# Attention's fill steps of an even unit all stand between its first and its second group of turned rows

## The chip, the cores and the metric

The kernel runs on one core of one Trainium2 chip. The metric is the device time of one execution in microseconds; the median of three timed runs is given, and one further execution was profiled.

## The reference, cut to what matters

Two layers, each with four token mixers beside each other on a sequence of 1024 tokens and a model width of 1024. Mixer A is softmax attention in a band, mixer C softmax attention over selected keys (here: all keys up to the query's tile, with a bias that masks those not selected). Both have four heads of width 64:

```python
# A: each 64-token chunk sees its own and 8 previous chunks
s = einsum('bnqhd,bnkhd->bhnqk', qc, kb) * dh ** -0.5 + bias
o = einsum('bhnqk,bnkhd->bnqhd', softmax(s), vb)
# C: the 256 best keys of an indexer
s = einsum('bqhd,bqkhd->bhqk', qb, ksel) * dh ** -0.5
o = einsum('bhqk,bqkhd->bqhd', softmax(s), vsel)
# both are multiplied by silu(z), projected, gated with sigmoids and summed
y = sum(sigmoid(g_b) * (o_b @ w_branch[b])); x = x + y @ w_out
```

B and D are recurrences in chunked form. All input projections and the sixteen blocks of gate columns are one matrix product `h @ w_in`, and that is most of the work.

## The kernel before, in words

All five engines run one program each, with semaphores between them. The order within an engine is written out by hand, and the engines run through the mixers in the order C, D, B, A, twice (two layers).

**Fills.** The large product `h @ w_in` is not a stage of its own. It is cut into *steps*, and `pe_fill(pe, n)` puts the next n steps into TensorE's stream wherever the hand-written order asks for them. During both attentions a step is one fp32 matmul of 128x128 by 128x512, which the profile shows as two MATMUL records of line 474. Four steps make a *product*: it accumulates in one of the two PSUM banks G, and when its last step is done ScalarE takes it out (lines 528, 537, 541, 547), for some products followed by a tanh (line 559) and a store. Seven products of this kind (`PRODUCTS`, p = 0 to 6) make one block of 256 columns. The lists of fills are handed to ScalarE by number: `act_ready(key)` first takes out every product that had ended, in TensorE's program order, when the job `key` was issued, and only then waits for `key` itself. So the place of a fill in TensorE's order also sets its place in ScalarE's order.

**Attention.** A *unit* u is one tile of 128 queries and one head; there are 32 (tile u // 4, head u % 4). TensorE's loop (line 1039 and after) takes for an even u the scores of units u and u+1 together (line 1003), into two double banks S2. VectorE adds the bias and takes the maximum (line 1102), line 1107 negates it, ScalarE takes the exponential (line 1083) and marks `probs`. TensorE then transposes ("turns") the probabilities of unit u in groups of at most four 128x128 tiles (line 1014), and ScalarE copies each group from PSUM (line 1069); then the values product follows (line 1027). There is one bank T for all turned groups, so a group can only be written when ScalarE has copied the one before it. In iteration u the loop turns the rows of unit u-1. A unit has a second group (`rest`) when it spans more than four key tiles. In mixer C unit u spans u // 4 + 1 tiles, so tiles 4 to 7 have a second group of 1 to 4 tiles; in mixer A it spans at most 5, so tiles 4 to 7 have a second group of one tile. Each finished tile is scaled and turned again through T (`oT`, line 1062).

In both mixers, VectorE's work on unit u waits for the last turned group of unit u-2 (it writes into the same buffer).

ScalarE's loop (line 1064 and after), in iteration u: copy of the first group of unit u-1; exponential of unit u; copy of the second group of unit u-1.

```python
ATT_FILL = {"A": 2, "C": 1}
ODD_FILL = {"A": 0, "C": 1}
```

Of the kernel before, what the change touches and what calls it, by code (L numbers as in the profile page):

```python
# [38 lines left out]
SEMS = 150  # L39
SMALL = 473  # L40

ATT_FILL = {"A": 2, "C": 1}
ODD_FILL = {"A": 0, "C": 1}
IDX_FILL = 1
A_FILL = 54
# [127 lines left out]
def gated_merge_kernel(nc, x, w_in, w_branch, w_out, params, toep, consts, cos_sin, a_mask, final_g, out):  # L173
    ctx = ExitStack()
    with ctx:
# [18 lines left out]
        C = lambda name: con[:, CONST[name][0]:CONST[name][1]]  # L194
# [41 lines left out]
        def sg(name):  # L236

            if name not in named:
                named[name] = ctx.enter_context(nc.semaphore(name))
            return named[name]  # L240
# [13 lines left out]
        for l in range(DEPTH):  # L254
# [52 lines left out]
            def next_unit():  # L307

                if todo:
                    b, js = todo[0]  # L310
                    free = fill_after.get((b, js[0])) is None or fill_after[b, js[0]] in jobs.at
                    if free:
                        todo.pop(0)
                        add_projection(b, js)
                        return True
                if gates[0] < len(gate_order):
                    add_gate()
                    return True
                return False

            def unit_at(key):

                return unit_of["gate", key[1]] if key[0] == "gate" else unit_of.get(key[:2])
# [96 lines left out]
            def pe_fill(pe, n):  # L420

                for _ in range(n):
                    if fill_at[0] == len(fills) and not next_unit():
                        return
                    key, blk, c, p = fills[fill_at[0]]
                    if unit_at(key) is None:
                        pe_fill_direct(pe, key, blk, c, p)
                    else:
                        pe_fill_product(pe, unit_at(key), key, c, p)
# [6 lines left out]
            def pe_fill_direct(pe, key, blk, m, c):  # L436

                slot, kt = 2 + blk % 2, fill_at[1]
                if kt == 0:
                    jobs.open(pe, key, next_g())  # L440
                    pe.wait_ge(sg(f"fill_w_loaded{blk % 2}"), 16 * (blk // 2 + 1))
                ap = jobs.at[key][0].ap
                ins = pe.matmul(ap, lhsT=wr[:, slot, kt, P * m:P * m + P], rhs=hT[:, kt, 512 * c:512 * c + 512],
                                start=kt == 0, stop=kt == KT - 1)
                fill_at[1] = kt + 1
                if kt == KT - 1:
                    pe_fill_ended(ins, key)

            def pe_fill_product(pe, u, key, i, p):

                h_side, w_side, fresh = PRODUCTS[p]
                kt = fill_at[1]
                if kt == 0:
                    jobs.open(pe, key, next_g())
                    if p == 0 and not i:
                        k = units[u][1][0]
                        pe.wait_ge(sg(f"fill_w_loaded{k % 2}"), 16 * (k // 2 + 1))
                    if p == 2 and u == 0:
                        pe.wait_ge(sg("h_sums"), 3)
                    if p == 3 and u == 0:  # L460
                        pe.wait_ge(sg("h_sums"), 5)
                    if w_side == "t2" and i == 0 and is_rows(u):
                        pe.wait_ge(sg("w_half_sums"), 2 * rows_units(u) + 2)
                    elif w_side in FIRST_T and not i:
                        pe.wait_ge(sg("w_sums"), 4 * u + FIRST_T[w_side])
                if is_rows(u) and w_side == "t2" and i == 0 and kt == half_k // 2:
                    pe.wait_ge(sg("w_sums"), 4 * u + 2)
                ap = jobs.at[key][0].ap
                if is_rows(u):
                    for kt in (kt, kt + 1):  # L470
                        ins = pe.matmul(ap[:, 0:NCB], lhsT=left(h_side, kt)[:, P * i:P * i + P], rhs=right(u, w_side)[:, kt, :],  # L471
                                        start=fresh and kt == 0, stop=kt == half_k - 1, skip_group_check=True)
                else:
                    ins = pe.matmul(ap, lhsT=right(u, w_side)[:, kt, :], rhs=left(h_side, kt), start=fresh and kt == 0,  # L474
                                    stop=kt == half_k - 1, skip_group_check=True)
                fill_at[1] = kt + 1
                if kt == half_k - 1:
                    pe_fill_ended(ins, key)
# [489 lines left out]
            def attention(b, q, k, v, z, first_tile, bias, at_s, at_pt, v_unit=None, each_unit=None, act_unit=None, masked=False):  # L968
# [7 lines left out]
                def span(u):  # L976
                    i, h = units[u]
                    k0 = first_tile(i)
                    return i, h, k0, i + 1 - k0
# [4 lines left out]
                def groups(nb):  # L984
                    return [(g, min(4, nb - g)) for g in range(0, nb, 4)]
# [10 lines left out]
                def scores(pe, u):  # L996

                    i, h, k0, nb = span(u)
                    aps = [jobs.open(pe, ("S", b, u + e), S2[e]) for e in range(2)]
                    for c in range(0, P * nb, 512):  # L1000
                        w = min(512, P * nb - c)
                        for e in range(2):
                            ins = pe.matmul(aps[e][:, c:c + w], lhsT=head(q, h + e, P * i, P * i + P),  # L1003
                                            rhs=head(k, h + e, P * k0 + c, P * k0 + c + w), start=True, stop=True)
                            if c + w == P * nb:
                                jobs.filled(ins, ("S", b, u + e))

                def turn(pe, u, group):

                    g, n = group  # L1010
                    key = ("PT", b, u, g)
                    ap = jobs.open(pe, key, T)
                    for j in range(n):
                        ins = pe.transpose(ap[:, P * j:P * j + P], rows[u % 2][:, P * (g + j):P * (g + j) + P], ident)  # L1014
                    jobs.filled(ins, key)
# [21 lines left out]
                def pe(pe):  # L1037
                    for u in range(len(units) + 2):
                        if u < len(units) and u % 2 == 0:
                            scores(pe, u)  # L1040
                        if 1 <= u <= len(units):
                            pe.wait_ge(sg("probs_" + b), u)
                            turn(pe, u - 1, groups(span(u - 1)[3])[0])
                        rest = groups(span(u - 1)[3])[1:] if 1 <= u <= len(units) else []
                        if u % 2 == 0:
                            pe_fill(pe, ATT_FILL[b])
                        elif not rest:
                            pe_fill(pe, ODD_FILL[b])
                        if u >= 3 and u % 2 == 1:
                            values(pe, u - 3)  # L1050
                        for group in rest:
                            turn(pe, u - 1, group)
                        if u % 2 == 0:
                            pe_fill(pe, ATT_FILL[b])
                        if u >= 5 and u % 4 == 1:
                            pe_fill(pe, 1)
                            i = u // 4 - 1
                            key = ("oT", b, i)
                            ap = jobs.open(pe, key, T)
                            pe.wait_ge(sg("z_scaled_" + b), i + 1)  # L1060
                            for m in range(2):
                                ins = pe.transpose(ap[:, P * m:P * m + P], z[:, i, P * m:P * m + P], ident)
                            jobs.filled(ins, key)
# [1270 lines left out]
```

## Time and profile before

| | us |
|---|---|
| median of 3 runs (2878.49 to 2882.49) | 2880.6 |
| the profiled execution | 2881.09 |
| its span in the trace | 2879.3 |
| TensorE busy in the span | 2790.9 (97%) |
| VectorE, ScalarE, GpSimd busy | 1584.4, 967.6, 819.7 |

The span runs from the first to the last recorded instruction; 1.8 us of the profiled time lie around it. "Busy" of TensorE contains modelled ends, so that a row's duration overlaps the start of the next row; the distance between two starts is what an instruction costs on TensorE. The attention of mixer C lies at about 350 to 458 us in layer 0 and 1785 to 1893 us in layer 1, that of mixer A at about 1059 to 1176 and 2492 to 2607 us.

### The profile page before, as it was taken

To read this page: it belongs to the slowest core of one execution; us is meant where nothing else is said; L and a number is where in the kernel's file an instruction comes from. 1 tells how busy PE (TensorE), PEld (TensorE's weight loads), DVE (VectorE), ACT (ScalarE), POOL (GpSimd) and SP (SyncE) were. 2 spreads that over 40 slices of the span, in tenths; PEclk is the share of its full clock that TensorE was granted. 3 is DMA by queue.
4 is the path that set the end of the run, shared out by engine and by line. 5 is a ranking of instruction groups with operands and counts; after the bars stand their busy time and mean duration, and the time that the engine had idled before them with its cause. 6 is when DMAs were issued, how large, how long until landed. Compare 5 with 4: busy or idle time off the path is not lost. (4 is left out here: it accounts for less than half of the span.)

```text
span 2879.3 us, 45819 instructions
## 1 busy us (share of the span) xinstructions
PE 2790.9 (97%) x18640; PEld 1493.9 (52%) x18640; DVE 1584.4 (55%) x2979; ACT 967.6 (34%) x1824; POOL 819.7 (28%) x578
## 2 busy tenths in 40 slices
PE   7999999999999999999999899999999999999998
PEld 4436444477644475444444364544776445654443
DVE  2788865633368813065227888656332787130743
ACT  3345764311143335300114457543111433352001
POOL 4323312321144232233052233123211443212330
PEclk9999999999999999999999999999999999999999
DMA  5212101111121221263042111011011212212731
GB/s 211 63 44 59 45 30 45 44 32 32 35 85 34 96 92 48 99 224 112 0 155 58 51 37 44 30 44 44 32 32 50 70 49 93 77 55 92 239 101 59
DMA packets 134985, 204.61 MB, mean 71 GB/s; under 512 B 8920, under 2 KB 88952, under 8 KB 134008
## 3 DMA queue, kind: packets, MB, share of 16 engines
q1 hardware_dynamic: 116184, 167.59, 18.5%
q10 hardware_dynamic: 18592, 34.09, 3.2%
q8 instruction: 149, 2.44, 0.4%
q14 instruction: 60, 0.49, 0.1%
HBM read 146.07 MB, written 48.78 MB: 68 GB/s over the span
## 5 line engine op out<-in xcount | busy, mean ns | idle before, releaser
L474 PE MATMUL ps<-hT,wr 128*128 128x512 f32 x1792 | 830.7, 601 | 3.6 <-ACT wr L528 2.0
L474 PEld LDWEIGHTS ps<-hT,wr 128*128 128x128 f32 x1792 | 326.7, 191 | 371.0 <-issue 354.7
L474 PE MATMUL ps<-sums,wr 128*128 128x512 f32 x896 | 431.3, 610 | 14.0 <-ACT arena L537 13.9
L634 POOL TENSOR_TENSOR gts<-gts,wr 128x512 f32<-128x512 f32 x96 | 138.0, 1437 | 572.0 <-ACT wr L528 349.4
L474 PEld LDWEIGHTS ps<-sums,wr 128*128 128x128 f32 x896 | 164.2, 194 | 192.8 <-issue 168.4
L1102 DVE CUSTOM_DVE_ANT_0 arena<-ps,arena 128x640 f32<-128x640 f32 (+7 forms) x128 | 90.4, 706 | 306.9 <-PE ps L1003 292.7
L713 PE MATMUL ps<-xo,arena 128*128 128x512 f32 x512 | 220.2, 592 | 1.6 <-ACT gts L541 1.6
L528 ACT ACTIVATE wr<-ps 128x512 f32<-128x512 f32 x168 | 99.6, 593 | 358.6 <-PE ps L474 315.4
L474 PE MATMUL ps<-wr 128*128 128x512 f32 x448 | 210.7, 599 | 1.3 <-ACT wr L528 1.3
L1485 DVE TENSOR_SCALAR_CACHE_REDUCE arena<-arena,sm 128x384 f32<-128x384 uint16 (+7 forms) x256 | 192.8, 809 | 2.2
L607 POOL TENSOR_TENSOR wr<-wr 128x512 f32<-128x512 f32 x62 | 84.7, 1365 | 363.6 <-PE ps L474 356.8
L1399 ACT ACTIVATE arena<-arena,sm 128x896 f32<-128x896 uint16 (+3 forms) x128 | 139.4, 1089 | 69.4 <-DVE sm L1481 69.1
L713 PEld LDWEIGHTS ps<-xo,arena 128*128 128x128 f32 x512 | 97.1, 190 | 124.7 <-issue 124.7
L880 ACT ACTIVATE arena<-arena 128x1024 f32<-128x1024 f32 x24 | 25.4, 1058 | 396.7 <-DVEq L959 392.3
L634 POOL TENSOR_TENSOR arena<-arena,wr 128x512 f32<-128x512 f32 x48 | 79.1, 1649 | 255.8 <-ACT wr L528 173.9
L537 ACT ACTIVATE arena<-ps 128x256 f32<-128x256 f32 (+1 forms) x144 | 68.4, 475 | 214.4 <-PE ps L474 101.7
L471 PE MATMUL ps<-wr,hT 128*128 128x256 f32 x576 | 139.1, 385 | 0.8 <-ACT arena L537 0.8
L1069 ACT ACTIVATE arena<-ps 128x512 f32<-128x512 f32 (+3 forms) x192 | 88.5, 461 | 140.3 <-PE ps L1014 138.7
L547 ACT ACTIVATE gts<-ps 128x512 f32<-128x512 f32 x96 | 57.0, 594 | 220.3 <-PE ps L474 203.4
L474 PEld LDWEIGHTS ps<-wr 128*128 128x128 f32 x448 | 81.1, 190 | 91.3 <-issue 85.8
L1458 DVE SCALAR_TENSOR_TENSOR arena<-arena,sm 128x512 f32<-128x512 f32 (+3 forms) x140 | 104.9, 749 | 28.9 <-ACT arena L1381 24.5
L471 PEld LDWEIGHTS ps<-wr,hT 128*128 128x128 f32 x576 | 106.3, 190 | 18.0 <-ACT arena L537 1.6
(308 smaller groups left out, 4366.8 us busy)
## 6 DMA issues: line engine op xcount, KB each, us to landing
wr<-in_w_in SPq DMA_DIRECT2D x68, 1024.0 KB, 5.3
gate_tanh<-gts ACTq DMA_DIRECT2D x128, 256.0 KB, 2.1
arena<-gate_tanh SPq DMA_DIRECT2D x128, 256.0 KB, 2.9
x_cur<-arena SPq DMA_DIRECT2D x2, 4096.0 KB, 23.0
arena<-in_w_branch SPq DMA_DIRECT2D x8, 1024.0 KB, 9.9
wr<-in_w_out SPq DMA_DIRECT2D x8, 1024.0 KB, 6.6
arena<-x_cur SPq DMA_DIRECT2D x4, 2048.0 KB, 8.8
arena<-arena SPq DMA_DIRECT2D x36, 128.0 KB, 2.8
```

The costliest lines, as they stand in the source:

```text
L471: ins = pe.matmul(ap[:, 0:NCB], lhsT=left(h_side, kt)[:, P * i:P * i + P], rhs=right(u, w_side)[:, kt, :], start=fresh and kt == 0, stop=k ...
L474: ins = pe.matmul(ap, lhsT=right(u, w_side)[:, kt, :], rhs=left(h_side, kt), start=fresh and kt == 0, stop=kt == half_k - 1, skip_group_ch ...
L528: jobs.emptied(act.activation(stage_of(u), src, ACT.Copy), key)
L537: jobs.emptied(act.activation(dest_of[key[:2]](i, slot), src, ACT.Copy), key)
L607: pool.tensor_tensor(t1[:, k0:], b12[:, k0:], b11[:, k0:], ALU.subtract).then_inc(sg("w_sums"), 1)
L634: pool.tensor_tensor(dst, dst, stage_of(u), ALU.add).then_inc(sg("pool_added"), 1)
L713: ins = pe.matmul(ap, lhsT=wbs[ORDER.index(b)][:, k2, P * ct:P * ct + P], rhs=xo[:, 2 * ORDER.index(b) + k2, 512 * half:512 * half + 512], ...
L1069: ins = act.activation(probs_t[u % 3][:, P * g:P * (g + n)], ap[:, 0:P * n], ACT.Copy)
L1102: ins = dve.tensor_tensor_reduce(out=rows[u % 2][:, 0:P * nb], in0=ap[:, 0:P * nb], in1=bias(i, h, nb), scale=HD ** -0.5, scalar=-3e38, op ...
L1399: act.activation(compared[i], half_keys(k // 16, i), ACT.Sign, bias=cand[:, j:j + 1], scale=-1.0, accum_out=count[:, j:j + 1]).then_inc(sg ...
L1458: ins = dve.scalar_tensor_tensor(acc, r, wgt, acc, ALU.mult, ALU.add)
L1485: ins = dve.tensor_scalar(compared[i], half_keys(part, i), cand[:, j:j + 1], None, ALU.is_lt, ALU.add, accum_out=count[:, j:j + 1])
```

## The change

The one number of fill steps per mixer becomes a pair: steps between the first group's turn and the second's, and steps behind the second's. An even iteration of A had 2 and 2 and gets 4 and 0; one of C had 1 and 1 and gets 2 and 0. The sum is the same. Where there is no second group (tiles 0 to 3) the order is the same as before. The one step of ODD_FILL and the one beside `oT` are not touched.

```diff
-ATT_FILL = {"A": 2, "C": 1}
+ATT_FILL = {"A": (4, 0), "C": (2, 0)}
 ...
                         if u % 2 == 0:
-                            pe_fill(pe, ATT_FILL[b])
+                            pe_fill(pe, ATT_FILL[b][0])
                         elif not rest:
                             pe_fill(pe, ODD_FILL[b])
                         if u >= 3 and u % 2 == 1:
                             values(pe, u - 3)
                         for group in rest:
                             turn(pe, u - 1, group)
                         if u % 2 == 0:
-                            pe_fill(pe, ATT_FILL[b])
+                            pe_fill(pe, ATT_FILL[b][1])
```

## Rows read from the trace of the kernel before

**Rows 1.** The page, part 1: busy us, share of the span, instructions.

```profile
PE 2790.9 (97%) x18640; PEld 1493.9 (52%) x18640; DVE 1584.4 (55%) x2979; ACT 967.6 (34%) x1824; POOL 819.7 (28%) x578
```

**Rows 2.** Stretches: length, busy PE, PEld, DVE, ACT, POOL, then PEclk, DMA.

```profile
348.00:456.00 108.00, 102.20 (x609) 53.17 (x607) 66.94 (x170) 64.25 (x143) 17.04 (x13) 1.00 0.08 25
456.00:700.00 244.00, 241.06 (x2719) 151.10 (x2718) 124.16 (x175) 63.72 (x115) 61.64 (x45) 0.97 0.13 42
...
2494.00:2610.00 116.00, 114.69 (x614) 61.86 (x615) 35.97 (x122) 60.72 (x151) 23.57 (x20) 1.00 0.18 66
```

**Rows 3.** Timeline, mixer A, layer 1, iteration 22: start, us, engine, line, [idle <-releaser].

```profile
2561.84 0.66 PE L1014 MATMUL ps<-con,arena 128*128 128x128 f32 x4
...
2562.33 1.02 PE L474 MATMUL ps<-sums,wr 128*128 128x512 f32 x2
...
2564.05 0.27 PE L1014 MATMUL ps<-con,arena 128*128 128x128 f32 x1
...
2564.38 0.28 ACT L1069 ACTIVATE arena<-ps 128x128 f32<-128x128 f32 x1
...
2565.32 0.15 DVE L1107 TENSOR_SCALAR sm<-sm 128x1 f32<-128x1 f32 x1
...
2565.88 0.60 PE L1014 MATMUL ps<-con,arena 128*128 128x128 f32 x4
...
2567.07 0.82 ACT L1083 ACTIVATE arena<-arena,sm 128x640 f32<-128x640 f32 x1
```

**Rows 4.** Timeline, mixer A, layer 1, iterations 26 and 27: around a product's end.

```profile
2582.03 0.60 ACT L547 ACTIVATE gts<-ps 128x512 f32<-128x512 f32 x1 [1.49 <-PE ps L474]
...
2582.52 0.62 ACT L559 ACTIVATE gts<-gts 128x512 f32<-128x512 f32 x1
2583.48 0.60 ACT L1069 ACTIVATE arena<-ps 128x512 f32<-128x512 f32 x1 [0.34 <-issue]
...
2584.13 0.33 PE L1014 MATMUL ps<-con,arena 128*128 128x128 f32 x1 [0.51 <-ACT arena L1069]
```

**Rows 5.** Timeline, mixer C, layer 0, iteration 28 (second group of three tiles).

```profile
438.10 0.66 PE L1014 MATMUL ps<-con,arena 128*128 128x128 f32 x4
...
439.50 0.31 PEld L1014 LDWEIGHTS ps<-con,arena 128*128 128x128 f32 x3 [0.71 <-ACT arena L1069]
439.50 0.55 PE L1014 MATMUL ps<-con,arena 128*128 128x128 f32 x3
...
440.80 0.47 ACT L1069 ACTIVATE arena<-ps 128x384 f32<-128x384 f32 x1
...
441.41 0.63 PE L1014 MATMUL ps<-con,arena 128*128 128x128 f32 x4 [0.51 <-ACT arena L1069]
```

**Rows 6.** Timeline, mixer C, layer 0: iterations 18, 22, 24, 26 and 30.

```profile
399.04 0.66 PE L1014 MATMUL ps<-con,arena 128*128 128x128 f32 x4
...
401.52 0.63 PE L1014 MATMUL ps<-con,arena 128*128 128x128 f32 x4
...
414.21 0.66 PE L1014 MATMUL ps<-con,arena 128*128 128x128 f32 x4
...
417.00 0.60 ACT L547 ACTIVATE gts<-ps 128x512 f32<-128x512 f32 x1
...
417.03 0.63 PE L1014 MATMUL ps<-con,arena 128*128 128x128 f32 x4
...
421.12 0.66 PE L1014 MATMUL ps<-con,arena 128*128 128x128 f32 x4
...
424.09 0.63 PE L1014 MATMUL ps<-con,arena 128*128 128x128 f32 x4 [0.26 <-ACT arena L1069]
...
433.46 0.63 PE L1014 MATMUL ps<-con,arena 128*128 128x128 f32 x4 [1.27 <-ACT arena L1069]
...
447.28 0.66 PE L1014 MATMUL ps<-con,arena 128*128 128x128 f32 x4
...
450.71 0.63 PE L1014 MATMUL ps<-con,arena 128*128 128x128 f32 x4 [0.50 <-ACT arena L1069]
```

## The prediction

> **What bounds the kernel now.** I read the page's busy shares first: TensorE is busy for 2790.9 us of 2879.3, the next engine for 1584.4 [rows 1]. So nearly every microsecond in which TensorE stands still is added to the end, and every other engine has room, unless TensorE waits for it. The stretches then say the same of the two attentions: 114.69 us of 116 in A's, 102.20 of 108 in C's, both at a granted clock of 1.00, and 241.06 of 244 in the stage that follows C, at 0.97 [rows 2]. A has hardly a gap to win; C has about 6 us per layer. The timeline says how one iteration goes, and that is where the change works.
>
> In A (iteration 22; G is the start of the first group's turn, 2561.84) the first fill step starts at G+0.49. Two steps later, at G+2.21, comes the second group's turn, so a step costs 0.86 us. The two steps behind the second group take as long, and the next first group starts at G+4.04, without a wait [rows 3]. What the reader is to see is ScalarE's row in between: the copy of the second group runs from 2564.38 to 2564.66, under those two steps. The next turn needs that copy finished, because both groups use bank T. The steps behind the second group are what hides this hand-over.
>
> In C (iteration 28) the same spot already has a wait. The step between the groups covers the first group's copy almost exactly: the second group starts at G+1.40 with no idle time on its MATMUL row. The next first group starts at G+3.31, with 0.51 us of idle time, because ScalarE copies the second group only after the exponential (0.47 us from 440.80) [rows 5]. The five other rows of C show where the next first group starts there: G+2.48, G+2.82, G+2.97 and G+3.43, and one with 1.27 us of idle time [rows 6].
>
> **What changes.** Only 32 places: iterations 18 to 32 (even) of each of four attentions, those where a second group exists. No instruction is added or taken away, and no DMA moves against another (the loads wait for products, whose order stays). At each place the second group's turn goes behind all the steps: 1.72 us later in A, 0.86 later in C. Directly behind it stands the next first group's turn, which waits for the second group's copy.
>
> *The bare hand-over.* From the start of the second group's turn to the next first group: the turn's own duration (0.27 for one tile, 0.60 for four, so 0.11 more per tile), 0.06 until ScalarE starts (2564.05+0.27 to 2564.38), the copy (0.28 for one tile [rows 3], 0.47 for three [rows 5], 0.60 for four [rows 4], 0.37 taken for two), and the time from the copy's end to TensorE's start. For this last part I have 0.14 (441.27 to 441.41 [rows 5]) and 0.05 (2584.08 to 2584.13 [rows 4]). I take 0.14, since that row is the same instruction in the same place.
>
> *A, a plain place.* 0.27 + 0.06 + 0.28 + 0.14 = 0.75, against the 0.11 that the turn costs when a fill follows. That is +0.64. It holds where no product ends in the last step: by nine steps per tile and four per product, iterations 18, 20, 22, 24 and 30. In 30 the product ends one step earlier and its evacuation is over in time. 5 x 0.64 = 3.2.
>
> *A, where a product ends late.* ScalarE serves products in program order. One that ended behind the second group was taken out after that group's copy; now it comes before. In iteration 28 (a product without a tanh) the evacuation starts 0.25 behind the last step's end (0.16 tail of the row, 1.02 against 0.86 [rows 3], and 0.09 until ScalarE starts), takes 0.60, overlaps the next row by 0.11 (2582.03+0.60 against 2582.52 [rows 4]), then copy 0.28 and 0.14: 1.16 in place of 0.11, or +1.05. In iteration 26 a tanh and two stores are issued too: the copy now starts 1.45 behind the evacuation (2582.03 to 2583.48 [rows 4]). The next first group then comes 0.25 - 0.11 + 1.45 + 0.28 + 0.14 = 2.01 later; the stop of 0.51 to 0.58 that is now behind the values goes away [rows 4], since the same evacuation is over by then. Net +1.45. In iteration 32 no first group follows, but the values wait for the copy; a product with a tanh ends one step before: the copy ends 0.67 after the steps, plus 0.05, against 0.17 now: +0.55. A in all: 3.2 + 1.05 + 1.45 + 0.55 = 6.25 per layer, 12.5 in two.
>
> *C.* New start of the next first group is G + 0.49 + 2 x 0.86 = G+2.21, plus the hand-over. For one tile (iteration 18) 2.96 against 2.48: +0.48. Two tiles (24): 3.16 against 2.97: +0.19. Three (28): 3.37 against 3.31: +0.06. Four (30): 3.61 against 3.43: +0.18 [rows 5, 6]. In iteration 22 a product ends in the second step; its evacuation (row at 417.00, behind the copy now) comes in front: 2.21 + 0.25 + 0.60 - 0.10 + 0.37 + 0.14 = 3.47 against 2.82: +0.65. In iterations 20 and 26 a product ends in the first step, so that evacuation (and in 26 a tanh) already stands before the copy, and ScalarE is the later one in both orders (the row with 1.27 us): 0. In iteration 32 the odd fill step of 0.86 follows and covers the copy: 0. Sum 1.56 per layer, 3.1 in two.
>
> *Cost put at nothing.* VectorE's work on the odd unit waits for the second group's turn, so it slides by the same 1.72 us in A. Its last row (2565.32+0.15) would end at 2567.19, and the exponential that needs it starts at 2567.07 now and 0.64 later after the change [rows 3]: 0.5 us of room. Were that gone, each plain place would cost up to 0.1 us for each 0.1 of overrun. The tail of every iteration (values, scores) has the same cover as before. The first group's copy gets more cover than it needs.
>
> **Sum.** 12.5 + 3.1 = 15.6, taken as 15.5. The profiled execution's 2881.1 would become 2896.6 (span 2879.3 to 2894.8). That execution lies 0.5 above the median of 2880.6, so the forecast is 2896. With 0.05 in place of 0.14 at some 26 hand-overs it would be 13.2; were every place in A as dear as iteration 26, 16 x 1.45 + 3.1 = 26.
>
> **The rivals.**
>
> *The bare hand-over is all.* Products that end late cost nothing extra (ScalarE gets them out in time), C is held by its exponential anyway, and the start is the quick one: 16 x 0.55 = 8.8, so 2889.4. For it: most of C's places have that hold. Against it: the strict order of ScalarE's list and the 1.45 in rows 4.
>
> *Nothing to measure.* The lost time is absorbed later, for instance in the stage behind C, where 3 us of 244 are idle [rows 2], or the next turn hardly waits: 2880.6. Against it: those waits hang on VectorE and ScalarE chains that start only when attention is done and slide along; A has no gaps.
>
> *Faster.* The weight-load row of C's second group shows 0.71 us of idle time before it, for bank T [rows 5]. There are 7 places per layer like it. If TensorE really stood still for that long, a second step in front of the group would win it: 14 x 0.71 = 9.9 us, and if in A the hand-over were hidden too, the time would be 2870.7. It decides for faster as soon as A loses under 9.9. Against it: the MATMUL row at that place has no idle time; the fill before it still runs while the load waits. What can truly be won is the 0.05 between copy and turn.
>
> *The clock falls.* In late A TensorE now runs without gaps at clock 1.00; after the change it stops for about half a microsecond or more every 8 us. C does that today, with stops of 0.26 to 1.27 us, and keeps 1.00 [rows 2, 5, 6]. If late A (some 66 us per layer) fell to the 0.97 of the stage behind C, that would add 132 x 0.03 = 4 us: 2900; if all of it ran at the lower of the two levels, up to 132 us.
> The Trainium skill (TensorE: Matmul & The Clock Gate, "A second HAM failure mode: psum-queue depth-cycling") warns that short idles between groups of matmuls, from cycling through PSUM banks, can make the clock go down and up again. By that rule this rival would be the likely one; the trace of C speaks against it here.
>
> **How the numbers follow.** Forecast (13 to 20 us added) 0.70; bare hand-over 0.11; nothing to measure 0.08; faster 0.03; the clock 0.04; a cost above 20 us without it 0.04. A measurement of this kernel tells about 0.2% (5.8 us) from no change. Slower takes in the forecast, the bare hand-over, the clock and the dear case, less a little: 0.88; same 0.09; faster 0.03. The range reaches down over the bare hand-over and up to the clock's small case: 2888 to 2902, which leaves out nothing to measure, faster and the far ends.
>
> **What would show it.** In the changed profile: in late A, the next first group at G+4.68 with idle time before it, released by line 1069; its second group at G+3.93; a copy of the second group right behind an evacuation in iterations 26 and 28; the 0.51 at the values' end gone; in C, first groups at G+2.96 to G+3.6 with nearly the same idle time as now, and those of iterations 20 and 26 unmoved; TensorE's busy time in A the same while the stretch is 6 us longer; stages B and D equally long. The prediction is wrong if VectorE's slide makes the exponential late (line 1083 waiting for line 1107 in A), if the granted clock in A leaves 1.00, or if the time lost in attention is found again behind it.

## The result and the profile after

The changed kernel takes 2893.86 us (median of 8 runs) against 2879.66 us of the kernel before (median of 8 runs, the three known ones among them). The recorded ratio, which is not exactly the quotient of the two medians, is 1.0051, with a 95% interval of 1.0035 to 1.0066. The medians differ by 14.2 us, where 15.5 were forecast. The profiled execution took 2890.21 us, its span is 2888.2.

The page after, part 1 [rows 1]:

```profile
PE 2786.6 (96%) x18640; PEld 1494.9 (52%) x18640; DVE 1580.8 (55%) x2979; ACT 968.8 (34%) x1824; POOL 820.7 (28%) x578
```

TensorE has the same 18640 instructions; it is not busier, it stands still longer. The stretches after (length, busy PE, PEld, DVE, ACT, POOL, then PEclk and DMA); the first is late mixer A in layer 1, from the exponential of unit 16 on, the second the stage behind C as in [rows 2]:

```profile
2542.00:2617.00 75.00, 69.49 (x407) 38.77 (x406) 20.80 (x65) 37.68 (x88) 11.36 (x9) 1.00 0.09 32
456.00:700.00 244.00, 241.07 (x2723) 151.01 (x2721) 123.67 (x175) 64.43 (x116) 61.04 (x45) 0.97 0.13 42
```

Late A now has 5.5 us without TensorE work in 75, and the granted clock is 1.00 all the same. The same work before, from the exponential of unit 16 to the last copy of `oT`, and then after:

```profile
2539.20:2607.44 68.24, 67.20 (x404) 38.30 (x403) 20.28 (x62) 36.71 (x88) 11.39 (x9) 1.00 0.10 36
2542.27:2616.29 74.02, 68.51 (x404) 38.39 (x403) 20.27 (x62) 37.03 (x87) 11.36 (x9) 1.00 0.10 33
```

The time in which TensorE stands went from 1.0 to 5.5 us; the stage is 5.8 longer. The stage behind C in layer 0 is as it was.

The timeline of iteration 22 of A in layer 1, after; it answers to [rows 3]:

```profile
2566.20 0.66 PE L1014 MATMUL ps<-con,arena 128*128 128x128 f32 x4
...
2566.70 1.02 PE L474 MATMUL ps<-sums,wr 128*128 128x512 f32 x2
...
2567.56 2.74 PE L474 MATMUL ps<-wr 128*128 128x512 f32 x6
...
2570.13 0.27 PE L1014 MATMUL ps<-con,arena 128*128 128x128 f32 x1
...
2570.44 0.28 ACT L1069 ACTIVATE arena<-ps 128x128 f32<-128x128 f32 x1 [1.59 <-PE ps L1014]
...
2570.86 0.63 PE L1014 MATMUL ps<-con,arena 128*128 128x128 f32 x4 [0.46 <-ACT arena L1069]
...
2571.40 0.15 DVE L1107 TENSOR_SCALAR sm<-sm 128x1 f32<-128x1 f32 x1
```

The second group stands at G+3.93 and the next first group at G+4.66, with 0.46 us of idle time that line 1069 ends. ScalarE had nothing to do for 1.59 us before the copy; the copy is not late, there is only nothing left to put under it.

Iteration 26 of the same stretch, after; it answers to [rows 4]:

```profile
2587.33 0.27 PE L1014 MATMUL ps<-con,arena 128*128 128x128 f32 x1
2587.53 0.60 ACT L547 ACTIVATE gts<-ps 128x512 f32<-128x512 f32 x1 [1.97 <-PE ps L474]
...
2588.02 0.62 ACT L559 ACTIVATE gts<-gts 128x512 f32<-128x512 f32 x1
2588.54 0.27 ACT L1069 ACTIVATE arena<-ps 128x128 f32<-128x128 f32 x1
2588.95 0.63 PE L1014 MATMUL ps<-con,arena 128*128 128x128 f32 x4 [1.35 <-ACT arena L1069]
```

The evacuation of a product (line 547) and a tanh (line 559) stand in front of a copy of 0.27 us, and the stop is 1.35 us. In C, layer 0, iterations 22, 24, 26 and 28 after, TensorE's line 1014 alone; they answer to [rows 5, 6]:

```profile
414.24 0.66 PE L1014 MATMUL ps<-con,arena 128*128 128x128 f32 x4
416.45 0.38 PE L1014 MATMUL ps<-con,arena 128*128 128x128 f32 x2
417.67 0.63 PE L1014 MATMUL ps<-con,arena 128*128 128x128 f32 x4 [0.84 <-ACT arena L1069]
...
421.76 0.66 PE L1014 MATMUL ps<-con,arena 128*128 128x128 f32 x4
...
424.92 0.63 PE L1014 MATMUL ps<-con,arena 128*128 128x128 f32 x4 [0.56 <-ACT arena L1069]
...
430.19 0.65 PE L1014 MATMUL ps<-con,arena 128*128 128x128 f32 x4
...
434.28 0.63 PE L1014 MATMUL ps<-con,arena 128*128 128x128 f32 x4 [1.38 <-ACT arena L1069]
...
438.91 0.66 PE L1014 MATMUL ps<-con,arena 128*128 128x128 f32 x4
...
442.28 0.63 PE L1014 MATMUL ps<-con,arena 128*128 128x128 f32 x4 [0.67 <-ACT arena L1069]
```

First group to first group these are 3.43, 3.16, 4.09 and 3.37 us, against 2.82, 2.97, 4.09 (429.37 to 433.46 in the trace before) and 3.31. Iteration 26 did not move: there ScalarE was the later one in both orders.

**Where the time went, in one measure.** The timed medians scatter by a few us; the trace does not. I take "late stage" as the time from the start of the exponential of unit 16 to the start of the last `oT` copy (line 927), and per iteration the distance of two even units' exponentials, all in us:

| late stage | C, layer 0 | A, layer 0 | C, layer 1 | A, layer 1 | sum |
|---|---|---|---|---|---|
| before | 68.79 | 67.79 | 68.78 | 68.24 | 273.60 |
| after | 70.19 | 74.02 | 70.20 | 74.02 | 288.43 |

| iteration | 16 | 18 | 20 | 22 | 24 | 26 | 28 | 30 to the end |
|---|---|---|---|---|---|---|---|---|
| A, layer 0, before | 8.11 | 7.35 | 8.43 | 7.35 | 8.55 | 7.48 | 8.43 | 12.09 |
| A, layer 0, after | 8.10 | 8.00 | 9.08 | 8.00 | 9.19 | 8.90 | 9.45 | 13.30 |
| C, layer 0, before | 7.52 | 6.07 | 9.23 | 6.95 | 8.26 | 8.85 | 9.19 | 12.72 |
| C, layer 0, after | 7.52 | 6.53 | 9.23 | 7.56 | 8.44 | 8.85 | 9.24 | 12.82 |

The four stages together are 14.8 us longer. The profiled span grew by only 8.9. Of the missing 5.9 us, 4.3 lie between the end of C and late A in layer 1 (645.1 us before, 640.8 after) and 1.3 in the same place in layer 0, where the granted clock was 0.50 for 13.7 us before and for 10.2 after. Here are the 106 us behind C in layer 1, before and then after, and below each the part in which they differ:

```profile
1894.00:2000.00 106.00, 104.86 (x252) 46.55 (x251) 76.02 (x80) 35.15 (x47) 38.13 (x23) 0.94 0.15 50
1903.50:1913.60 10.10, 10.10 (x13) 3.50 (x12) 9.82 (x13) 4.11 (x6) 0.00 (x0) 0.50 0.00 0
```

```profile
1901.00:2007.00 106.00, 104.26 (x269) 46.81 (x267) 80.68 (x83) 37.48 (x54) 39.38 (x23) 0.98 0.15 49
1910.80:1920.90 10.10, 10.10 (x23) 3.76 (x23) 9.82 (x13) 4.72 (x7) 1.07 (x1) 1.00 0.07 26
```

The change doesn't touch this code; the execution after gets more of it done in 106 us. In the execution before, TensorE ran for 10.2 us at a granted clock of 0.50, the lower of the two levels (1.2 of 2.4 GHz), and started 13 matmul records where the execution after started 23 at full clock. By the mean granted clocks of 0.94 and 0.98 that is an estimated 4 us. The runs speak against the change as the cause: the other eight traces of this document all have a stretch of 10.2 to 13.7 us at 0.50 in this place, among them one with both mixers in the changed order (10.2 us). Nor do the timed runs differ in it: the mean granted clock of the 8 runs after is 0.9908, that of 29 runs of the kernel before is 0.9907. The clock goes with the scatter between runs instead. Over those 29 the time falls as the mean clock rises (correlation -0.93): the fastest (2870.25 us) had a mean clock of 0.994, the slowest (2885.72) 0.988.

### The profile page after: what moved, and what is told of

It reads as the page before. It is cut to its first block, busy times and chain, and to the rows that moved or that the text cites. A ratio compares the mean times of both kernels' runs of the same rounds, so it can differ in the third digit from the quotient of the medians.

```text
span 2888.2 us, 45827 instructions
## 1 busy us (share of the span) xinstructions
PE 2786.6 (96%) x18640; PEld 1494.9 (52%) x18640; DVE 1580.8 (55%) x2979; ACT 968.8 (34%) x1824; POOL 820.7 (28%) x578
## 4 chain that ended last, share of the span: by engine, by line
PE 39%; DVE 6%; ACT 2%; DMA 1%; issue 1%; POOL 1%; SPq 0%; DVEq 0%; ACTq 0%; POOLq 0%
PE ps L474 19%; PE ps L713 4%; PE ps L471 4%; PE ps L727 3%; DVE arena L1485 1%; PE ps L1003 1%; PE ps L1014 1%; PE ps L1856 1%; PE ps L1358 1%; PE ps L1027 1%; DVE arena L1743 1%; DMA x_cur<-arena 1%; PE ps L1904 1%; PE ps L1848 0%; DMA wr<-in_w_in 0%
## 5 line engine op out<-in xcount | busy, mean ns | idle before, releaser
L1014 PE MATMUL ps<-con,arena 128*128 128x128 f32 x528 | 95.0, 284 | 24.1 <-ACT arena L1069 23.3
```

## The experiments

The two tables' measure is used for all. For each run the recorded ratio to the kernel before is given with its interval. It is taken against 29 runs of that kernel from the same session (median 2882.22 us for the first four experiments, 2881.09 for the last four), not against the 8 above.

**Mixer A alone.**

```diff
-ATT_FILL = {"A": (4, 0), "C": (2, 0)}
+ATT_FILL = {"A": (4, 0), "C": (1, 1)}
```

> Mixer A has the changed order (4, 0), mixer C the old one (1, 1). Theory (the bare hand-over of bank T, 0.64 us at a plain place of A, plus ScalarE taking out a late product first): 6.25 us per layer, so +12.5 us or a ratio of 1.0043, and iteration 22 of A at 4.68 us from one first group to the next in place of 4.04. Rival, the time comes from somewhere else than A's hand-over (the clock or C): clearly less than 9 us, or a granted clock under 1.00 in A's stretch.

Measured: 2892.49 us, ratio 1.0049 (1.0033 to 1.0065). A's late stages are 74.02 and 74.01, C's 68.78 and 68.79. So A alone costs 6.2 and 5.8 us, and the granted clock of its stretch stays at full:

```profile
1108.00:1184.00 76.00, 70.49 (x416) 39.41 (x415) 21.35 (x66) 37.64 (x89) 11.35 (x9) 1.00 0.09 32
```

**Mixer C alone.**

```diff
-ATT_FILL = {"A": (4, 0), "C": (2, 0)}
+ATT_FILL = {"A": (2, 2), "C": (2, 0)}
```

> Mixer C has the changed order (2, 0), mixer A the old one (2, 2). Theory: C's exponential already holds the next first group, so 1.4 to 1.56 us per layer, +3 us or a ratio of 1.0011, and iterations 20 and 26 of C exactly as long as before. Rival, the wait of the weight load (0.71 us, 7 places per layer) was a real stop of TensorE: faster by up to 9.9 us, ratio 0.9966.

Measured: 2881.96 us, ratio 1.0009 (0.9998 to 1.0020). C's late stages 70.19 and 70.19: +1.4 us each, with iterations 20 and 26 at 9.23 and 8.85 as before. The interval includes no difference, so that C's cost rests on the stages and not on the medians. The 0.71 us in front of the weight loads were no stop of TensorE: in this run they are gone, and no iteration is shorter for it.

**One step behind the second group.**

```diff
-ATT_FILL = {"A": (4, 0), "C": (2, 0)}
+ATT_FILL = {"A": (3, 1), "C": (1, 1)}
```

> Mixer A with three steps between the groups and one behind, mixer C as of old. Theory: one step of 0.86 us covers the hand-over of 0.64 us, so the plain places cost nothing; only iteration 30, where a product ends in the third step and is taken out ahead of the second group's copy, loses about 0.2 us. In all 0 to 0.5 us per layer, ratio 1.000 (to 1.0004). Rival, the loss is in proportion to how far the second group is moved (VectorE's slide): half of A's loss, about +6 us, ratio 1.002.

Measured: 2881.31 us, ratio 1.0005 (0.9993 to 1.0016). A's late stages 68.51 and 68.52; iterations 18 to 28 are 7.35, 8.43, 7.36, 8.54, 7.49 and 8.43 in layer 0, to 0.01 as before. So 0.86 us of work cover the hand-over whole, though the group was moved by half as far, and the loss isn't in proportion to the move; VectorE's work on the odd unit, which was moved too, costs nothing here. The 0.72 us per layer are all in iterations 30 and 32 (12.81 in place of 12.09), where a product ends in the third step: 0.14 in iteration 30 and 0.57 in iteration 32. I had reckoned with 0.2 in iteration 30 alone and left out iteration 32. There the copy, and with it the values product, waits for an evacuation and a tanh (timeline, iteration 32, layer 0):

```profile
1174.32 0.60 ACT L528 ACTIVATE wr<-ps 128x512 f32<-128x512 f32 x1 [1.92 <-PE ps L474]
1174.82 0.62 ACT L559 ACTIVATE gts<-gts 128x512 f32<-128x512 f32 x1
1175.34 0.27 ACT L1069 ACTIVATE arena<-ps 128x128 f32<-128x128 f32 x1
1175.75 1.31 PE L1027 MATMUL ps<-arena 128*64 128x128 f32 x20 [0.49 <-ACT arena L1069]
```

**The second group into another bank, changed order.** There is no spare bank; but of the two fill banks only one holds a product under way.

```diff
                     key = ("PT", b, u, g)
-                    ap = jobs.open(pe, key, T)
+                    ap = jobs.open(pe, key, G[(gcount[0] + 1) % 2] if g else T)
```

> The changed order in both mixers, but the second group is turned into that of the two fill banks G in which no product is under way, in place of bank T. Theory: the next first group no longer waits for the second group's copy; plain places of A go back to 4.04 us; what is left in A is the values' wait for a copy behind a late product (iterations 26, 28, 32: some 1.8 us per layer), and C gets shorter than before by about 3 us per layer, since the first group waits for the exponential alone. In all about 3 us under the kernel before, ratio 0.998 to 1.000, and 17 us under the changed kernel. Rival, VectorE's later start or the clock is what costs: the time stays at 1.004 or more.

Measured: 2884.03 us, ratio 1.0015 (1.0005 to 1.0024). The late stages are C 66.54 and 68.18, A 70.38 and 70.38, in all 1.9 us above the kernel before and 13 below the changed one. The hand-over was through bank T: iterations 18 and 22 of A fall from 8.00 to 7.40, next to the 7.35 of before. The expected total, 3 us under the kernel before, was too low by some 5 us. Most of it is that I had taken the fill bank as free. It isn't where a product follows at once. In iteration 17 of C the second group lies in that bank until ScalarE has done the exponential, which waits for VectorE. First layer 0, TensorE alone, then layer 1:

```profile
397.99 1.12 PE L474 MATMUL ps<-hT,wr 128*128 128x512 f32 x2 [1.72 <-ACT arena L1069]
```

```profile
1832.11 0.83 ACT L1083 ACTIVATE arena<-arena,sm 128x640 f32<-128x640 f32 x1 [0.26 <-DVE sm L1107]
...
1832.94 0.26 ACT L1069 ACTIVATE arena<-ps 128x128 f32<-128x128 f32 x1
1833.25 1.97 PE L474 MATMUL ps<-hT,wr 128*128 128x512 f32 x2 [1.71 <-ACT arena L1069]
```

The fill step waits 1.7 us in both layers: the wait has moved from the turn to the fill.

Layer 1 pays more for it, and this is a place where the clock does fall. The same step takes 1.97 us there and 1.12 in layer 0, because the granted clock is down from 1833.4 on:

```profile
1833.40:1836.80 3.40, 3.40 (x8) 1.42 (x10) 0.61 (x1) 0.38 (x1) 0.00 (x0) 0.50 0.00 0
```

The lower level lasts for 3.4 us and makes iteration 16 of layer 1 10.07 us long, against 8.43 in layer 0: 1.6 of the missing 5 us. It is the only fall within an attention in the ten traces. TensorE stood for 1.71 us before it; after a stop of 1.72 in layer 0 the clock stayed at 1.00.

**The copy ahead of the products, changed order.** ScalarE only waits for a second group, and takes out ended products afterwards.

```diff
-                        ap = act_ready(act, ("PT", b, u, g))
+                        ap = (jobs.ready if g else act_ready)(act, ("PT", b, u, g))
```

> The changed order; ScalarE only waits for a second group and copies it, and takes out products that ended before it afterwards. Theory: the part of the loss that comes from evacuations in front of the copy goes away, the bare hand-over stays. Per layer, A: iteration 28 from +1.02 to +0.64, iteration 26 about 0.8 less, iteration 32 about 0.1 less, the plain places unchanged at +0.64. C: iterations 20, 22 and 26 shorter by about 0.35, 0.3 and 0.9. In all some 5 to 6 us under the changed kernel. Rival, it is the hand-over alone in all places: no difference from the changed kernel (+14 us over the kernel before).

Measured: 2891.35 us, ratio 1.0040 (1.0024 to 1.0056). The late stages are C 68.45 and 68.46, A 72.72 and 72.71: 6.1 us under the changed kernel. The plain places of A stay at 8.00, 9.08, 8.00 and 9.19. In layer 0 iteration 26 falls from 8.90 to 8.00 and iteration 28 from 9.45 to 9.08; iterations 30 and 32 together fall by only 0.03 (13.29 to 13.26). In C iterations 20, 22 and 26 are 0.72, 0.28 and 0.71 shorter. Iterations 20 and 26 had not lost anything by the change, so their 2.9 us in two layers are a wait that the kernel before has too; 3.2 us are left as the products' part of the change. The timeline of iteration 26 of A, layer 1:

```profile
2590.33 0.28 ACT L1069 ACTIVATE arena<-ps 128x128 f32<-128x128 f32 x1 [2.08 <-PE ps L1014]
2590.50 0.59 ACT L547 ACTIVATE gts<-ps 128x512 f32<-128x512 f32 x1
2590.75 0.63 PE L1014 MATMUL ps<-con,arena 128*128 128x128 f32 x4 [0.46 <-ACT arena L1069]
```

The copy comes first and the stop is 0.46 us, the one of a plain place, in place of 1.35.

**The copy ahead of the products, old order.** The same edit of ScalarE's list on the kernel before.

> The order of before, with ScalarE taking out a second group ahead of products that ended before it. Theory: in C, iteration 20 loses 0.4 and iteration 26 0.9 us of TensorE's wait (product in front of the second group's copy), A is unchanged because its steps behind the group cover the evacuation: 1.3 us per layer, 2.6 in all, ratio 0.9991. Rival, the product's evacuation is then late for something else (the next product's bank): no gain.

Measured: 2876.41 us, ratio 0.9987 (0.9978 to 0.9995). C's late stages are 67.05 and 67.05, 1.7 us less each: iterations 20 and 26 go from 9.23 to 8.51 and from 8.85 to 7.85. A is 67.78 in both layers, which is the kernel before without the late stores of layer 1 (see below). The gain in iteration 20 was expected at 0.4 and is 0.72. This is the one version that is faster than both kernels with an interval that leaves out no difference. Iteration 26 of C, where [rows 6] has a stop of 1.27 us:

```profile
430.53 0.47 ACT L1069 ACTIVATE arena<-ps 128x384 f32<-128x384 f32 x1
430.90 0.59 ACT L528 ACTIVATE wr<-ps 128x512 f32<-128x512 f32 x1
431.14 0.63 PE L1014 MATMUL ps<-con,arena 128*128 128x128 f32 x4 [0.27 <-ACT arena L1069]
```

**The idle fill bank for C's even iterations only, old order.**

```diff
-                    ap = jobs.open(pe, key, T)
+                    ap = jobs.open(pe, key, G[(gcount[0] + 1) % 2] if g and b == "C" and u % 2 else T)
```

> The order of before in both mixers; in C the second group of even iterations is turned into the idle fill bank, everything else in T. Theory: C's next first group waits for the exponential alone: about 3.3 us less per layer in C (iterations 18 to 30: 0, 1.2, 0.3, 0.3, 0.4, 0.45, 0.55), and iteration 16 stays at 7.52 us; A exactly as before. In all -6.5 us, ratio 0.9977. Rival, TensorE then waits for the fill bank to be emptied at the next product (as it does for 1.7 us in one place of the kernel with both kinds of second groups there): less than half of this.

Measured: 2879.86 us, ratio 1.0000 (0.9990 to 1.0010): a miss. C's late stages are 67.89 and 67.90, 0.9 us less each in place of 3.3. Iterations 18, 22, 24 and 28 gain 0.2 to 0.4 and the end 0.6, but 20 gains nothing and 26 goes from 8.85 to 9.69. In both a product starts in the step behind the second group and needs the same bank. In iteration 26 TensorE then stands for 2.15 us, and the granted clock stays at 1.00. Iteration 20:

```profile
409.33 0.58 ACT L528 ACTIVATE wr<-ps 128x512 f32<-128x512 f32 x1
409.81 0.27 ACT L1069 ACTIVATE arena<-ps 128x128 f32<-128x128 f32 x1
...
410.12 1.13 PE L474 MATMUL ps<-sums,wr 128*128 128x512 f32 x2 [1.39 <-ACT arena L1069]
```

**The same with C's two steps together.** The bank as in the run before, ATT_FILL with (2, 2) for A and (2, 0) for C.

> As the run before, but mixer C with its two steps together (2, 0); A as before the change. Theory: once the hand-over does not pass through T, the order of the steps in C matters little: C within 0.5 us per layer of the run before, ratio 0.998. If the steps together were good in themselves (fewer changes between fills and turns), it would be the faster of the two by more than that; if VectorE's later start on the odd unit costs, it would be slower by more.

Measured: 2878.24 us, ratio 0.9997 (0.9988 to 1.0005). C's late stages are 68.12 and 68.11, 0.2 us from the run before. Iteration by iteration the two differ: 26 is 1.2 us shorter (8.48 against 9.69), the end 1.0 longer (13.18 against 12.16), as the start of the next product falls before or behind the second group. So the sums agree within the 0.5 us that was expected, but through differences of 1.2 and 1.0 us that cancel. It is not shown that the order of C's steps matters little in itself once the hand-over is not through T; nor can this pair of runs tell what fewer changes between fills and turns, or VectorE's later start, are worth. That C would be some 3 us per layer shorter than before was wrong here as in the run before.

## Why the prediction was right

**The bound** held: the late stages account for 14.8 us and the medians differ by 14.2. The profiled span grew by 8.9 alone, which looks like the sign of being wrong that the prediction names, time found again behind the attention. The traces put most of it down to the lower clock of the one execution before, as shown above, and not to an absorption.

**The bare hand-over** was forecast at 0.64 us per plain place of A and is 0.65 in iterations 18, 20, 22 and 24 (7.35 to 8.00, 8.43 to 9.08, 8.55 to 9.19). The second group came at G+3.93 as stated, the next first group at G+4.66 for G+4.68. The bank experiment shows that bank T carries the wait, and the (3, 1) experiment that one step covers it.

**A product in front of the copy** was forecast at +1.05 for iteration 28 (measured 1.02), +1.45 for iteration 26 (1.42 in layer 0) and +0.55 for iteration 32 (0.56); 30 and 32 together, forecast at 1.19, came to 1.21. The experiment that turns only ScalarE's order around takes 0.90 back in iteration 26 and 0.37 in iteration 28, which brings 28 to the 0.65 of a plain place. In iteration 32 it takes back next to nothing: the values' product still waits for 0.46 us there, so that this term was the bare hand-over and not the product in front.

The hit in iteration 26 was luck. The forecast took 1.45 us from the evacuation to the copy, and 0.51 to 0.58 of a stop that would go away, both from [rows 4] in layer 1. In that execution the issue of the two stores took 1.35 us there, as ScalarE's row shows, against 0.81 in layer 0 and in both layers after. Layer 0, then layer 1, both before:

```profile
1151.57 0.81 ACTq L565 DMA_DIRECT2D gate_tanh<-gts  x2
...
2582.08 1.35 ACTq L565 DMA_DIRECT2D gate_tanh<-gts  x2
```

After the change the evacuation and the copy are 1.01 us apart (2587.53 to 2588.54), and from one first group to the next the loss is 1.51 us, not 2.01, in both layers. In layer 0 the two errors cancel, since only 0.14 of a stop was there to go away. In layer 1, where 0.58 went away, the iteration lost 0.97. So A was forecast at 6.25 and measured 6.23 and 5.78; without the late stores, which lengthened the stage before by 0.45, it would be 6.2 in both.

**C** was forecast at 1.56 per layer and measured 1.40 and 1.42. Its iterations: 18 +0.46 (forecast 0.48), 20 0.00 (0), 22 +0.61 (0.65), 24 +0.18 (0.19), 26 0.00 (0), 28 +0.05 (0.06), 30 and 32 together +0.10 (0.18). The last is the only term a little off: iteration 30 alone lost 0.17, as forecast, and in iteration 32 the values start 0.07 sooner behind the first group (3.61 against 3.68 us), which the forecast had put at 0.

**VectorE's slide**, put at nothing, is nothing: its wait for the second group is there (line 1107 starts at 2571.40, G+5.20 in place of G+3.48, as worked out), and the exponential it feeds still comes after it, at 2572.08, since ScalarE has the first group's copy to do until then.

**The rivals.** The hand-over alone (8.8 us) falls: the products' part is 3.2 us, a plain place costs 0.65 and not 0.55, and C loses where this rival had nothing. "Nothing to measure" and "faster" fall with the stages. The clock stays at 1.00 in late A with a stop of 0.46 to 1.35 us at each place.
The warning of the Trainium skill (TensorE: Matmul & The Clock Gate, "A second HAM failure mode: psum-queue depth-cycling") is about bf16 matmuls of 512 columns; for the stops of the changed kernel the trace does not agree with it.
But the clock rival is not empty. The run with the other bank shows 3.4 us at 0.50 behind a stop of 1.71 us, and its 12 runs have a mean granted clock of 0.9892 where the kernel before has 0.9907. Stops of 1.72 and 2.15 us elsewhere left the clock alone, so that the length of the one stop doesn't decide, and what does stays open.

The ratio of the A-only run (1.0049) looks like that of the whole change, but the intervals are as wide as C's share (1.0009). The means of its session differ by 11.8 us (2892.34 for its 6 runs, 2880.57 for 29 of the kernel before), next to the 12.0 of its stages.

## What to carry to other kernels

Filler work belongs behind the instruction whose result must be handed over, not in front of it: in A one step of 0.86 us behind a turned group hid a hand-over of 0.64 us, and four in front hid nothing of it. When two engines share one order of service, look at what stands in the list in front of the short thing that the bounding engine waits for: putting a copy of 0.3 to 0.5 us ahead of an evacuation of 0.6 us was worth 3.5 us here (two places in each C), with no instruction more. A borrowed buffer moves a wait to its owner; see who opens it next before counting the gain.

## What the runs showed of the hardware that was not expected

From the end of ScalarE's copy to the start of what waits for it on TensorE there are two values, about 0.14 and about 0.05 us. Over the late attentions of the ten traces, 0.13 to 0.15 stands at all 157 groups of four tiles that waited (2570.44+0.28 to 2570.86 above), and at the values' products. About 0.05 stands at second groups of one tile (21), at the turns of `oT` (32) and at the fill steps in the borrowed bank (12), as in 1832.94+0.26 to 1833.25 above. The length of the wait doesn't decide: 0.05 follows waits of 0.15 to 2.15 us, 0.14 waits of 0.16 to 1.38. It goes by the kind of instruction; why is not shown.

The stretch behind C in layer 1 ran at a granted clock of 0.50 for 10.2 to 13.7 us in nine of ten traces and not at all in the tenth, which makes some 4 us, nearly a third of this change. Stage lengths inside attention agree between executions to 0.02 us in most places, so the stages decided what the medians alone could not. The exception is iteration 26 of A in layer 1, which took from 7.48 to 8.09 us in the five traces where A has its old order.
